# A modulation product of two vectors, moved from TensorE to VectorE between the tiles of a projection

## What is computed

```python
# first block, each of 2 layers: feed-forward part
hm = rms_norm(x, g_mlp)
x = x + jnp.square(jax.nn.relu(hm @ w_up)) @ w_down          # 1024 -> 4096 -> 1024
# second block: modulation, for the tokens (mod_l) and for the context (mod_c)
mod_l = jax.nn.silu(c) @ w_mod[l] + b_mod[l]                  # 1024 -> 6 * 1024
mod_c = jax.nn.silu(c_ctx)[None, :] @ w_mod[l] + b_mod[l]
sh1, sc1, g1, sh2, sc2, g2 = jnp.split(mod_l, 6, axis=-1)
sh1c, sc1c, g1c, sh2c, sc2c, g2c = jnp.split(mod_c, 6, axis=-1)   # only sh1c, sc1c are used
```

## Time and profile before

| | |
|---|---|
| runs | 1579.18 us median of 3 (1578.57 to 1581.71) |
| the profiled execution | 1582.1 us, its span 1580.3 us |
| instructions | 17826 |
| stage with the first layer's up and down projection | about 219 to 408 us of the span |
| the same of the second layer | about 616 to 806 us |
| expert weights, DMA at 410 to 430 GB/s | from about 1100 us to the end |

### The profile page before, as it was taken

One profiled execution on the slowest core, in us unless ns is written; L12 is line 12 of the kernel. 1 busy time (PEld: TensorE's weight loads), 2 busy tenths in 40 slices (PEclk: granted clock), 3 DMA queues, 4 the chain that ended last, 5 costly groups with the idle time before them and its releaser, 6 DMA issues.

```text
span 1580.3 us, 17826 instructions
## 1 busy us (share of the span) xinstructions
PE 1434.2 (91%) x7537; PEld 1015.2 (64%) x7537; DVE 582.3 (37%) x885; ACT 555.4 (35%) x713; POOL 676.0 (43%) x187
## 2 busy tenths in 40 slices
PE   8999999999999999999999999999996676676666
PEld 6877788877887778887788888977842121121111
DVE  4632423336263242334753686768510010010001
ACT  6356444433535645434343433574310000000001
POOL 5946587755784658786565774110000000000000
PEclk9999999999999999999999999999998788788788
DMA  8535357588553445659825354113999999999997
GB/s 295 183 112 160 136 184 237 175 303 303 182 185 131 140 148 182 228 181 334 319 88 184 122 151 149 34 68 124 410 413 429 426 428 429 428 428 428 428 428 293
DMA packets 115516, 395.38 MB, mean 250 GB/s; under 512 B 5719, under 2 KB 9620, under 8 KB 101996
## 3 DMA queue, kind: packets, MB, share of 16 engines
q1 hardware_dynamic: 113372, 388.70, 65.9%
q0 software_dynamic: 1520, 4.49, 0.8%
q10 hardware_dynamic: 544, 1.05, 0.2%
HBM read 393.16 MB, written 1.05 MB: 249 GB/s over the span
## 4 chain that ended last, share of the span: by engine, by line
PE 70%; DMA 23%; DVE 2%; ACT 2%; POOL 1%; issue 1%; SPq 1%; DVEq 0%; ACTq 0%
PE psum L2283 16%; PE psum L2285 16%; PE psum L2284 16%; DMA ring<-in_w_e_down 7%; PE psum L1241 7%; DMA ring<-in_w_e_gate 6%; DMA ring<-in_w_e_up 6%; PE psum L1156 2%; DMA ring<-in_w_down 2%; PE psum L2436 1%; DMA hT<-in_w_mod 1%; PE psum L2463 1%; DMA ring<-in_w_in 1%; PE psum L1017 1%; PE psum L2512 1%; POOL ring_lo L657 1%
## 5 line engine op out<-in xcount | busy, mean ns | idle before, releaser
L657 POOL TENSOR_TENSOR ring_lo<-ring,ring_hi 128x2048 fp32r<-128x2048 f32 x118 | 540.7, 4590 | 231.9 <-ACT ring_hi L637 231.8
L2285 PE MATMUL psum<-ring_hi,hT_hi 128*128 128x512 f32 (+2 forms) x912 | 352.8, 387 | 0.0
L637 ACT ACTIVATE ring_hi<-ring 128x2048 fp32r<-128x2048 f32 (+1 forms) x127 | 239.8, 1889 | 321.4 <-DMA ring<-in_w_down 108.8
L2284 PE MATMUL psum<-ring_lo,hT_hi 128*128 128x512 f32 (+2 forms) x912 | 352.2, 386 | 0.0
L2283 PE MATMUL psum<-ring_hi,hT_lo 128*128 128x512 f32 (+2 forms) x880 | 348.6, 396 | 1.7 <-DVE arena L2675 1.1
L1241 PE MATMUL psum<-arena 128*32 128x512 f32 x796 | 143.9, 712 | 64.1 <-DMA arena<-in_w_e_down 23.6
L2285 PEld LDWEIGHTS psum<-ring_hi,hT_hi 128*128 128x128 f32 x912 | 171.4, 188 | 35.0
L2283 PEld LDWEIGHTS psum<-ring_hi,hT_lo 128*128 128x128 f32 x880 | 165.5, 188 | 41.2 <-issue 6.0
L2284 PEld LDWEIGHTS psum<-ring_lo,hT_hi 128*128 128x128 f32 x912 | 171.8, 188 | 31.1
L1241 PE MATMUL psum<-ring,arena 128*32 128x512 f32 x720 | 134.1, 734 | 57.2 <-DMA ring<-in_w_e_gate 23.1
L1241 PEld LDWEIGHTS psum<-arena 128*32 128x32 f32 x796 | 32.4, 127 | 165.5 <-issue 74.5
(11 more groups left out here) (463 smaller groups left out, 1798.7 us busy)
## 6 DMA issues: line engine op xcount, KB each, us to landing
ring<-in_w_in SPq DMA_DIRECT2D x59, 1024.0 KB, 5.2
ring<-in_w_up SPq DMA_DIRECT2D x32, 1024.0 KB, 5.5
ring<-in_w_down SPq DMA_DIRECT2D x32, 1024.0 KB, 5.8
ring<-in_w_e_down SPq DMA_DIRECT2D x16, 2048.0 KB, 20.0
arena<-in_w_e_up SPq DMA_DIRECT2D x14, 2048.0 KB, 20.8
arena<-in_w_e_down SPq DMA_DIRECT2D x12, 2048.0 KB, 22.2
ring<-in_w_e_gate SPq DMA_DIRECT2D x12, 2048.0 KB, 22.7
arena<-in_w_e_gate SPq DMA_DIRECT2D x12, 2048.0 KB, 22.9
```

Of the source, the lines that this page charges most:

```text
L637: act.activation(slot_hi(u)[:, 0:c, :], slot(u)[:, 0:c, :], ACT.Copy).then_inc(hi_sb, 1)
L657: eng.tensor_tensor(slot_lo(u)[:, 0:c, :], slot(u)[:, 0:c, :], slot_hi(u)[:, 0:c, :].bitcast(F32), ALU.subtract).then_inc(done, 1)
L2284: pe.matmul(dst, hi(k0 + k), w_lo, start=False, stop=False)
L2285: last = pe.matmul(dst, hi(k0 + k), w_hi, start=False, stop=stop and k == nk - 1)
```

## The change

Group 0 too is now weighed on VectorE, for both vectors (`weigh_first`): for each slot 8 instructions, 4 chunks times 2 vectors, summed in SBUF in `mod_row` (for `c`) and in the new `ctx_row` (for `c_ctx`). Slots 0 and 1 are weighed after the instructions of up-projection tiles 4 and 5 (in the loop, n is 4 or 5), slot 3 after the low part of unit 50, slot 2 before that of unit 54; in the second layer the context's small steps come between the two. TensorE sums group 0 after unit 53 by 8 matmuls: `one_column` is 32 columns of zeros, one of ones and 31 of zeros, and a window into it puts the sum of `mod_row` into row 0 and that of `ctx_row` into row 1. The third group's sums move from after unit 59 to after unit 60. Loads: group 1's slots 0 and 1 now go behind units 47 and 49 and wait for the weighing of group 0's slots 0 and 1, its slot 3 behind unit 54, its slot 2 behind unit 56; slot 3 of a group comes before slot 2 and has a semaphore of its own (`x_in`). `ctx_junk`, the unused result of the context's squares, moves from SBUF to PSUM, because `ctx_row` takes its place.

```diff
...
 LO_VECTOR = [(l, u) for l in range(DEPTH) for u in SPLIT if (l == 0 and u < 2) or (u >= 50 and u % 4 == 2)]
-WEIGHED = [(l, q) for l in range(DEPTH) for q in (1, 2)]
-MOD_LOADS = {40: (0, (0,)), 43: (0, (1,)), 52: (0, (3,)), 53: (0, (2,)), 55: (1, (0, 1)), 56: (1, (2,)), 57: (1, (3,)),
-             58: (2, (0, 1)), 59: (2, (2, 3))}
-MOD_STEPS = (51, 56, 59)
-MOD_SUMS = 16 * len(WEIGHED)
+MOD_ORDER = (0, 1, 3, 2)
+MOD_LOADS = {40: (0, (0,)), 43: (0, (1,)), 47: (1, (0,)), 49: (1, (1,)), 51: (0, (3,)), 53: (0, (2,)), 54: (1, (3,)), 56: (1, (2,)),
+             58: (2, (0, 1)), 59: (2, (3,)), 60: (2, (2,))}
+MOD_STEPS = (53, 56, 60)
+MOD_SUMS = 64 * DEPTH
+
+def summed(l, q, j):
+    return 64 * l + (0, 32, 48)[q] + (8, 4, 4)[q] * (MOD_ORDER.index(j) + 1)
+
 LO_POOL = [(l, u) for l in range(DEPTH) for u in SPLIT if (l, u) not in LO_VECTOR]
...
         silu_c = silu_wide[:, 0:DEPTH * UC * 32].rearrange("p (l c n) -> p l c n", l=DEPTH, c=UC)
+        one_column = silu_wide[:, 256:320]
...
         mod_slot = [carve(16384, UC, UN), xn[:, :, :].rearrange("p t (c n) -> p (t c) n", n=UN), carve(18432, UC, UN),
                     hT[:, :, :].rearrange("p k t -> p (k t)").rearrange("p (c n) -> p c n", n=UN)]
         mod_row = carve(27648, 4, UN)
+        def ctx_row(l, j):
+            return carve(20480 + UN * j if l + 1 == DEPTH or j < 2 else 23808 + UN * (j - 2), UN)
         r_up = carve(18432, 2, TT, UN)
...
-        ctx_junk = [carve(20480 + D * t, D) for t in range(TT)]
+        ctx_junk = [flat[2 + t] for t in range(TT)]
...
                                 sp.dma_start(mod_acc[m:m + 97:32, q, :], row).then_inc(bias_in, 16)
                     if u in MOD_LOADS:
                         q, slots = MOD_LOADS[u]
-                        if q == 1:
-                            sp.wait_ge(mod_full, l * 3 + 1)
-                        elif q == 2:
-                            sp.wait_ge(mod_sb, 16 * WEIGHED.index((l, 1)) + 4 * slots[-1] + 4)
+                        if q:
+                            sp.wait_ge(mod_sb, summed(l, q - 1, slots[-1]))
                         for j in slots:
                             c0 = UN * (4 * q + j)
                             sp.dma_start(mod_slot[j], w["w_mod_2"][0].rearrange("(h c p) n -> h p c n", h=DEPTH, p=P)[l, :, :, c0:c0 + UN])\
-                              .then_inc(mod_in if j < 2 else rest_in, 16)
+                              .then_inc((mod_in, mod_in, rest_in, x_in)[j], 16)
             sync_block2(sp, load)
...
                 if u >= U_EX:
                     s, rounds = EX_ARRIVAL[u - U_EX]
-                    before = U8 // R1 if s < R1 else 1 if s < R1 + PIECES or s in (R + 13, R + 14) else 8 if s == R + 15 else 0
+                    before = U8 // R1 if s < R1 else 1 + 3 * DEPTH if s == R + 13 else 1 if s < R1 + PIECES or s == R + 14 else 8 if s == R + 15 else 0
                     pe.wait_ge(slot_in[s] if s < R else more_in[s - R], 16 * (rounds + before))
                 elif u >= U_OUT:
                     pe.wait_ge(lo_v, PIECES + len(LO_VECTOR) + u - U_OUT + 1)
...
                         for q in range(3):
                             if u != MOD_STEPS[q]:
                                 continue
+                            pe.wait_ge(mod_sb, summed(l, q, MOD_ORDER[-1]))
                             if q == 0:
-                                pe.wait_ge(silu_sb, 3)
-                                pe.wait_ge(u_lo, l * 8 + 8)
-                            pe.wait_ge(mod_in, l * 96 + 32 * (q + 1))
-                            pe.wait_ge(rest_in, 16 + l * 96 + 32 * (q + 1))
-                            if (l, q) in WEIGHED:
-                                pe.wait_ge(mod_sb, 16 * WEIGHED.index((l, q)) + 16)
+                                pe.wait_ge(cleared, 2)
+                                for m in range(2):
+                                    for j in range(4):
+                                        last = pe.matmul(psum[32 * j:32 * j + 32, 4, :], one_column[:, 32 - m:64 - m],
+                                                         ctx_row(l, j) if m else mod_row[:, j, :], start=m == 0, stop=m == 1)
+                            else:
                                 for j in range(4):
                                     rows = mod_row[:, j, :] if q == 1 else mod_slot[j][:, UC - 1, :]
                                     last = pe.matmul(psum[32 * j:32 * j + 32, 4 + q, :], const("ones"), rows, start=True, stop=True)
-                            else:
-                                for k in range(UC):
-                                    for j in range(4):
-                                        last = pe.matmul(psum[32 * j:32 * j + 32, 4 + q, :], silu_c[:, l, k, :], mod_slot[j][:, k, :],
-                                                         start=k == 0, stop=k == UC - 1)
                             last.then_inc(mod_full, 1)
                         if l + 1 == DEPTH and u == 56:
                             pe.wait_ge(mod_add, 3 * l + 1)
...
                     dve.tensor_tensor(uT_lo[:, k, :], flat[2 + n % 2].rearrange("p (k t) -> p k t", k=4), uT_hi[:, k, :].bitcast(F32),
                                       ALU.subtract).then_inc(u_lo, 1)
+                def slot_arrived(q, j):
+                    if j < 2:
+                        dve.wait_ge(mod_in, 32 * (3 * l + q + 1))
+                    else:
+                        dve.wait_ge(rest_in if j == 2 else x_in, 16 * (3 * l + q + 2))
+                def weigh_first(j):
+                    slot_arrived(0, j)
+                    if l == 0:
+                        dve.wait_ge(silu_sb, 3)
+                    count = summed(l, 0, j) - 8
+                    for k in range(UC):
+                        for m in range(2):
+                            total = ctx_row(l, j) if m else mod_row[:, j, :]
+                            own = silu_c[:, l, k, m:m + 1]
+                            if k:
+                                dve.wait_ge(mod_sb, count - 1)
+                                dve.scalar_tensor_tensor(out=total, in0=mod_slot[j][:, k, :], scalar=own, in1=total,
+                                                         op0=ALU.mult, op1=ALU.add).then_inc(mod_sb, 1)
+                            else:
+                                dve.tensor_scalar(total, mod_slot[j][:, k, :], own, None, ALU.mult).then_inc(mod_sb, 1)
+                            count += 1
+                def weigh_mod(q, j):
+                    slot_arrived(q, j)
+                    count = summed(l, q, j) - 4
+                    part = psum[:, 4 + q, :]
+                    for k in range(UC):
+                        own = silu_c[:, l, k, 0:1]
+                        rows = mod_slot[j][:, k, :]
+                        dve.wait_ge(mod_sb, count)
+                        if k == 0:
+                            dve.tensor_scalar(part, rows, own, None, ALU.mult).then_inc(mod_sb, 1)
+                        else:
+                            if k == UC - 1 and q == 1 and j == MOD_ORDER[0]:
+                                dve.wait_ge(mod_full, l * 3 + 1)
+                            total = mod_row[:, j, :] if q == 1 else rows
+                            dve.scalar_tensor_tensor(out=part if k < UC - 1 else total, in0=rows, scalar=own, in1=part,
+                                                     op0=ALU.mult, op1=ALU.add).then_inc(mod_sb, 1)
+                        count += 1
                 for n in range(8):
                     dve.wait_ge(slots_free, l * UNITS1 + unit_done(33 + 2 * n if n else 34))
                     if n >= 2:
...
                                                  op0=ALU.mult, op1=ALU.mult).then_inc(up_sb, 1)
                     if n:
                         low_squares(n - 1)
+                    if n in (4, 5):
+                        weigh_first(n - 4)
                 low_squares(7)
-                def weigh_mod(q, slots, arrived, first):
-                    dve.wait_ge(arrived, first + l * 96 + 32 * (q + 1))
-                    if q == 1 and l == 0:
-                        dve.wait_ge(silu_sb, 3)
-                    count = 16 * WEIGHED.index((l, q)) + 4 * slots[0]
-                    if q == 1:
-                        dve.wait_ge(mod_full, l * 3 + 1)
-                    part = psum[:, 4 + q, :]
-                    for j in slots:
-                        for k in range(UC):
-                            own = silu_c[:, l, k, 0:1]
-                            rows = mod_slot[j][:, k, :]
-                            if count:
-                                dve.wait_ge(mod_sb, count)
-                            if k == 0:
-                                dve.tensor_scalar(part, rows, own, None, ALU.mult).then_inc(mod_sb, 1)
-                            else:
-                                total = mod_row[:, j, :] if q == 1 else rows
```

(18 more changed lines are left out.)

## The result

The changed kernel takes 1588.86 us at the median of 7 executions (1584.88 to 1594.73), the kernel before 1581.71 beside it: ratio 1.0057, interval [1.0045, 1.0068] (estimated over all executions; the two medians alone give 1.0045). It is slower, as forecast, and inside the wide range of 1582 to 1612, but by 7 us here, and 11 in a second measurement, and not by 22; the narrower 1594 to 1608 is missed. The spread is part of the result: the seven executions of the kernel before lie within 4 us, these within 10 us.

What follows compares the result with a forecast made beforehand. TensorE, busy 91% of the span, was taken as the bound, with GpSimd's supply line nearly full. Layers +11.2 and +9.4 us plus 1.5 for the clock made +22 on 1579.2: 1601 us, own range 1594 to 1608, wide range 1582 to 1612.

Steps and rivals of the forecast that it cites:

- nothing collides: Rival, 11%: VectorE's instructions don't wait for GpSimd's subtractions, slots take 5.8 us each, and the kernel gets faster, 1575 us.
- Saved: Group 0's sums on TensorE: fewer matmuls, the new sum 1.94 us, sparing 1.7 us in each layer, 3.4 in all.
- Step 1: Slot 0 behind tile 4: VectorE's instructions wait out GpSimd's subtractions, so it takes 21.6 us and not 5.8.
- Step 2: Tile 5's instructions queue behind slot 0 on VectorE, so TensorE waits 5.2 us for them before the transposes.
- Step 3: Unit 48's load, issued 8 us late behind SyncE's wait, makes its low part late: TensorE waits 1.1 us.
- Step 4: Slot 1, weighed while GpSimd is idle until unit 48 is there: 5.8 us, nothing on the path.
- Step 5: Slots 3 (19 us) and 2 before the sums: TensorE waits 2.4 us, second layer 4.2; unit 54's low part 0.3.
- Step 6: SyncE waits for slot 3 behind unit 54, so unit 55 is late: 4.4 us, second layer 1.2.
- The clock: TensorE's granted clock falls after long waits, 2.5 us lost each; 1.5 us taken in all, bounds 0 and 10.
- milder: Rival, 12%: SyncE's waits are short and only the wait for the sums costs, +4 to +6 per layer, 1588 us.

Runs made afterwards that it cites:

- after_again: The changed kernel measured once more with no edit, for a second trace and interval: 1591.98 us, 1.0068 of the kernel before.
- loads_late: The changed kernel with group 1's loads moved behind units 54, 55, 56 and 57: 1593.45 us, 1.0072 of the kernel before.
- psum_late: The changed kernel with the running sums of slots 3 and 2 kept in PSUM: 1586.01 us, 1.0038 of the kernel before.

## Why the prediction was right and wrong

The sign and the mechanism were right, and "nothing collides" is out: instructions of 737 to 5104 ns on one line. The size was off by a factor of two to three, 7 and 11 us where 22 was forecast. By my steps:

- *Saved, 1.7 us per layer, 1.94 for the new sum*: right, 1.94 measured.
- *Step 1, slot 0 in 21.6 us*: 16.0 in the first trace, 20.3 in after_again. I counted two instructions per gap, three in the longest; three went through gaps of 0.86 and 1.33, two through 0.63, one through 0.35. I also took 0.78 us from one instruction to the next, and it is 0.68. Six instructions through the first two gaps, against five, and two through the third: that is the whole difference. My own count was not even followed: 2, 3 and 2 make seven by 297 us, so that the slot ends near 302.2 and not 303.6, and TensorE's wait comes to 3.7 us and not 5.2. That is what after_again has.
- *Step 2, 5.2 us in each layer*: **the step that failed.** Slot 0 needs the third gap or the fourth, and tile 5's cover ends between the two. I priced it as certain; it is 0 or 3.5 to 4.0 us, by a gap's 0.3 us. In the profiled execution the term is 0, of the forecast 10.4 in two layers; the trace of the second measurement has 7.5.
- *Step 3, 1.1*: 0. SyncE stood 7.9 us, but unit 48 left only 2 us late and not 8; the landing of 7.5 was right (7.4 from issue to rounding). The term does not follow from its own parts either: 304.1 + 7.5 + 1.9 + 4.6 is 318.1, before the 319 at which TensorE wants it, and not 320.
- *Step 4, slot 1 in 5.8 us, nothing on the path*: right (5.5), and for the reason given, that GpSimd is idle. loads_late shows what it costs when it isn't. I wrote that both tensor inputs of all the new instructions lie in SBUF; 16 of the 64 are TENSOR_SCALAR with one, and they collide as well (up to 4.84 us).
- *Step 5, slot 3 in 19, slot 2 in 5.8, sums waiting 2.4 and 4.2*: 17.9 and 4.9; the sums wait 0 and 0.5. Slot 3 began 6.5 us earlier than I had it, since the delays of steps 2 and 3 that I carried forward weren't there. With 7 us less in front, the same slot is covered. Unit 54's 0.3 us was 0.4.
- *Step 6, 4.4 and 1.2*: 1.9 and 1.2, by the same chain.
- *The clock, +1.5, bounds 0 and 10*: 0 behind the waits of the first trace. Where a wait was followed by a fall, the per-wait size (2.5) was about right, 1.4 to 2.5 measured.

So one misjudged count, instructions per gap, was carried through steps 2, 3, 5 and 6, which are one chain and not five terms: +20.6 became +0.4 at 1035 us in the first trace; after_again stands 7.6 us behind that trace near 1070 us, with 7.5 us of waits at the transposes and 1.4 of clock. Seven of 14 timed executions lie above 1590 us; the two medians are 7 and 11 us over the kernel before. Of the rivals *milder*, at 1588 us with 12%, was right in size; its reason (SyncE's waits short) was not, as SyncE stood 7.9 us. What my rivals lacked was a case with two outcomes: one mechanism just on either side of its cover.

What stays open: why gaps of GpSimd differ by 0.3 us between executions of one kernel (a subtraction that VectorE holds up ends 0.2 to 0.6 us later and so shortens the gap behind it, but the moments at which ScalarE ends them differ as well), and how many of the untraced executions have one wait, how many two. Neither was tried.

## What to carry to other kernels

Before moving work to an engine with idle time, look at where its operands will be: the same accumulation beside GpSimd costs 0.75 us an instruction with its running sum in PSUM and up to 5.1 in SBUF, 42 us on this kernel. Work put in front of something that TensorE needs should be cut so small that the worst collision still ends within the cover; halving two slots took away the 5 us of wait per layer of loads_late without removing an instruction. And when delays are summed, keep those of one chain as one term with its threshold, since each is there only if the one ahead of it is.

## What the runs showed that I had not expected

- VectorE gets three instructions through a GpSimd gap of 0.70 or 0.86 us, two through 0.61 and one through 0.35, and the next subtraction then mostly lasts 4.8 to 5.2 us instead of 4.6. GpSimd pays at most 0.6 us per collision, VectorE up to 4.4 (5.1 less the 0.74 of its own).
- A queue that stands can shield: with SyncE's stand of 7.9 us and the load behind it moved, the kernel did not gain (1.0072), since unit 48's subtraction came 4.7 us earlier and brought a subtraction under slot 1.
- The granted clock stayed at 1.00 behind a wait of 3.5 us and fell behind one of 4.0 in the same execution; behind one of 3.7 in psum_late it fell for longer than behind either of the longer ones.
